# Loading two weight tiles ahead of x, and using both on each block of x: the start of a fused attention layer on one Trainium2 core

## The reference, cut to what matters

```
h = x @ w_in + b_in                      # w_in is 1024 x 5376
q_a, k_a, v_a, gate_a, q_b, k_b, v_b, gate_b, mg_a, mg_b = split(h)
o_a = sliding_window_attention(rope(q_a), rope(k_a), v_a, sinks) * silu(gate_a)
o_b = stick_breaking_attention(q_b, k_b, v_b) * silu(gate_b)
merged = sigmoid(mg_a) * (o_a @ w_up_a) + sigmoid(mg_b) * (o_b @ w_up_b)
out = layer_norm(alpha * x + merged @ w_out)
```

## Time and profile before

| what | value |
|---|---|
| median of 3 timed executions | 861.12 us (857.84 to 861.34) |
| span of the profiled execution | 860.0 us |
| PE busy | 802.8 us, 93% of the span |
| POOL, DVE, ACT busy | 369.3, 465.4, 352.0 us |
| mean granted TensorE clock | 0.982 |
| DMA moved | 51 MB, 59 GB/s over the span |

### The profile page before, as it was taken

The page is one execution under the profiler, slowest core; times in us unless marked ns, Lnnn a source line. Parts: engine busy times, 40 slices in busy tenths (PEclk is TensorE's granted clock), DMA queues, the critical chain, the costliest instruction groups (busy, mean ns, idle before and its releaser), DMA issues.

```text
span 860.0 us, 10173 instructions
## 1 busy us (share of the span) xinstructions
PE 802.8 (93%) x3872; PEld 659.7 (77%) x3872; DVE 465.4 (54%) x620; ACT 352.0 (41%) x644; POOL 369.3 (43%) x321
## 2 busy tenths in 40 slices
PE   8999999999879987998899888999999999999996
PEld 6887877787767776777777666888888888888885
DVE  6377555375886588658865887411202202254453
ACT  7587454543545344534453445312111111144220
POOL 0222111235696669666866687322122222210392
PEclk9999999999999999999999999999999999999999
DMA  9141100013001200120022000111111111124251
GB/s 329 39 123 32 42 27 26 29 48 96 1 25 42 82 1 26 52 71 0 25 59 65 0 26 26 50 50 50 49 50 50 50 49 50 50 72 173 75 204 65
DMA packets 16912, 51.01 MB, mean 59 GB/s; under 512 B 2272, under 2 KB 2272, under 8 KB 16864
## 3 DMA queue, kind: packets, MB, share of 16 engines
q1 hardware_dynamic: 16864, 50.37, 17.7%
HBM read 40.92 MB, written 4.19 MB: 52 GB/s over the span
## 4 chain that ended last, share of the span: by engine, by line
PE 65%; POOL 21%; issue 7%; DVE 4%; ACT 2%; DMA 1%; POOLq 0%; SPq 0%; ACTq 0%; DVEq 0%
PE ps L78 20%; PE ps L80 20%; PE ps L79 20%; POOL keep L313 7%; POOL beta L309 5%; POOL o_t L327 3%; POOL sig_m L322 3%; POOL w_lo L289 2%; PE ps L1139 1%; PE ps L1122 1%; PE ps L1207 1%; PE ps L1150 1%; DVE stick_a L880 1%; ACT w_hi L402 1%; DVE beta L889 1%
## 5 line engine op out<-in xcount | busy, mean ns | idle before, releaser
L289 POOL TENSOR_TENSOR w_lo<-raw,w_hi 128x1024 fp32r<-128x1024 f32 (+1 forms) x53 | 120.2, 2268 | 348.5 <-ACT w_hi L402 347.7
L78 PE MATMUL ps<-x_hi,w_hi 128*128 128x512 f32 x672 | 267.6, 398 | 1.5 <-DVE x_lo L797 1.5
L80 PE MATMUL ps<-x_hi,w_lo 128*128 128x512 f32 x672 | 263.5, 392 | 0.0
L79 PE MATMUL ps<-x_lo,w_hi 128*128 128x512 f32 x672 | 263.3, 392 | 0.0
L78 PEld LDWEIGHTS ps<-x_hi,w_hi 128*128 128x128 f32 x672 | 127.9, 190 | 27.9 <-DVE x_lo L797 2.4
L80 PEld LDWEIGHTS ps<-x_hi,w_lo 128*128 128x128 f32 x672 | 127.0, 189 | 27.6
L79 PEld LDWEIGHTS ps<-x_lo,w_hi 128*128 128x128 f32 x672 | 127.5, 190 | 24.6
L975 DVE TENSOR_TENSOR sig_m<-sig_m,ps 128x512 f32<-128x512 f32 x16 | 10.9, 681 | 168.1 <-PE ps L80 168.1
L402 ACT ACTIVATE w_hi<-raw 128x1024 fp32r<-128x1024 f32 x49 | 51.9, 1060 | 113.3 <-PE ps L80 112.9
L1176 PE MATMUL ps<-ident,beta 128*128 128x128 f32 x288 | 49.9, 291 | 37.8 <-DVE w_t L896 30.1
L567 ACT ACTIVATE w_t<-ps 128x512 fp32r<-128x512 f32 (+1 forms) x96 | 46.6, 490 | 89.5 <-PE ps L1176 89.0
(11 more groups left out here) (112 smaller groups left out, 1183.9 us busy)
## 6 DMA issues: line engine op xcount, KB each, us to landing
raw<-in_w SPq DMA_DIRECT2D x56, 512.0 KB, 3.2
o_t<-in_xt SPq DMA_DIRECT2D x16, 256.0 KB, 5.7
ks<-ks SPq DMA_DIRECT2D x16, 256.0 KB, 4.3
raw<-in_xn SPq DMA_DIRECT2D x8, 512.0 KB, 3.5
out<-o_t SPq DMA_DIRECT2D x16, 256.0 KB, 2.0
raw<-in_w SPq DMA_DIRECT2D x4, 256.0 KB, 5.5
ka<-ka SPq DMA_DIRECT2D x4, 256.0 KB, 4.3
o_t<-in_cos SPq DMA_DIRECT2D x1, 512.0 KB, 5.2
```

The source lines that it names most:

```text
L78: pe.matmul(out, w_hi, x_hi, start=first, stop=False)
L79: pe.matmul(out, w_hi, x_lo, start=False, stop=False)
L80: return pe.matmul(out, w_lo, x_hi, start=False, stop=last)
L289: pool.tensor_tensor(w_lo[:, n % 2, cols], raw[:, n % 2, cols], w_hi[:, n % 2, cols].bitcast(F32), ALU.subtract).then_inc(lo_first if part ...
```

## The change

The first halves of tiles 0 and 1 are now the first two DMAs, ahead of all of x, and their second halves go out together before block 2. ACT and DVE split them in that order. On PE a new function `first_tiles(h)` waits for each block of x and multiplies it with K_A and then with V_A, in two PSUM banks that fill side by side; the order K_A, V_A, K_A, V_A over the halves becomes both on half 0, both on half 1. What follows, and what waits for it, is untouched.

```
-            sp.dma_start(raw[:, 0, 0:HALF], w[0][:, 0:HALF]).then_inc(first_in[0], 16)
+            for n in range(2):
+                sp.dma_start(raw[:, n, 0:HALF], w[n][:, 0:HALF]).then_inc(first_in[n], 16)
             for h in range(2):
                 cols = slice(HALF * h, HALF * (h + 1))
                 for k in range(KT):
                     if h == 0 and k == 2:
-                        sp.dma_start(raw[:, 0, HALF:D], w[0][:, HALF:D]).then_inc(raw_in[0], 16)
+                        for n in range(2):
+                            sp.dma_start(raw[:, n, HALF:D], w[n][:, HALF:D]).then_inc(raw_in[n], 16)
                     sp.dma_start(o_t[:, k, cols], xt[k][:, cols]).then_inc(x_in[KT * h + k], 16)
                 if h == 0:
-                    sp.dma_start(raw[:, 1, 0:HALF], w[1][:, 0:HALF]).then_inc(first_in[1], 16)
-                    sp.dma_start(raw[:, 1, HALF:D], w[1][:, HALF:D]).then_inc(raw_in[1], 16)
...
             first_weights_hi(0, 0)
+            first_weights_hi(1, 0)
             for h in range(2):
                 for k in range(KT):
                     if h == 0 and k == 2:
                         first_weights_hi(0, 1)
+                        first_weights_hi(1, 1)
                     act.wait_ge(x_in[KT * h + k], 16)
...
-                if h == 0:
-                    first_weights_hi(1, 0)
-                    first_weights_hi(1, 1)
...
+            def first_tiles(h):
+
+                xs = slice(HALF * h, HALF * (h + 1))
+                for k in range(KT):
+                    pe.wait_ge(x_lo_done, KT * h + k + 1)
+                    for n in (K_A, V_A):
+                        if h == 0 and k == 0:
+                            pe.wait_ge(first_lo, n + 1)
+                        if h == 0 and k == 4:
+                            pe.wait_ge(lo_done, n + 1)
+                        wk = slice(P * k, P * (k + 1))
+                        last = mma3(pe, ps[:, 2 * n + h, :], w_hi[:, n, wk], w_lo[:, n, wk], x_hi[:, k, xs],
+                                    x_lo[:, k, xs], k == 0, k == KT - 1)
+                        if k == KT - 1:
+                            last.then_inc(half_done, 1)
+
             for h in range(2):
-                for n in (K_A, V_A):
-                    chunk(n, 2 * h)
-                    chunk(n, 2 * h + 1)
+                first_tiles(h)
```

More of the change, by code:

```diff
@@ L791, in _ @@
             first_weights_lo(0, 0)
+            first_weights_lo(1, 0)
             for h in range(2):
@@ L795, in _ @@
                         first_weights_lo(0, 1)
+                        first_weights_lo(1, 1)
                     dve.wait_ge(x_hi_done, KT * h + k + 1)
@@ L798, in _ @@
                                       ALU.subtract).then_inc(x_lo_done, 1)
-                if h == 0:
-                    first_weights_lo(1, 0)
-                    first_weights_lo(1, 1)
             dve.wait_ge(const_in, 32)
```

## The result

| | before | after |
|---|---|---|
| first comparison, median | 859.48 us (4 runs) | 865.62 us (4 runs) |
| ratio | | 1.007, 95% interval 1.0042 to 1.0097 |
| the same kernel again, 5 rounds | 859.8 us | 865.6 us |
| ratio | | 1.0071, interval 1.0055 to 1.0088 |
| span of the profiled execution | 860.0 us | 861.8 us |

The change makes the kernel slower by 0.7%, 6.1 us. 865.0 was forecast, against 861.12 then shown for the kernel before. With more executions of it that one came to 858.2 to 859.8, so the change costs more than the 3.9 to 4.5 us that were forecast. A time and a span are not the same number: in every execution for which both are known the time is 1.7 to 1.8 us above the span (863.51 and 861.8 in the changed kernel's profiled execution). The 860.0 that served as the forecast's lower base was a span and no second estimate of the time.

The account below looks back on a forecast made before the run. PE was taken to bound the kernel, busy for 93% of the span. Start +0.1, wait +3.2 and clock +1.2 made +4.5 us, on 860.0 or 861.12; 865.0 us was forecast, range 863 to 866.5.

Parts of the forecast that it names:

- The wait behind it: Before Q_A (tile 2), PE waits 3.2 us for POOL's w_lo, since tile 0's slot comes free too late.
- What PE waits for elsewhere: PE's waits before the change: 37.6 us in the stick-breaking stage, 1.5 at line 1139, 1.17 and 0.34 for x.
- The covers behind it: After Q_A's start, V_A's eviction and the next tile's weight_hi stay hidden, by 3 us and more.
- The clock after the wait: PE's low clock following the wait before Q_A costs +1.2 us, between bounds of 0 and 1.7.
- Start +0.1: First two tiles: PE starts at 7.9, not 5.64, and ends at 31.4 against 31.32, +0.1 us.
- the gain at the front is nil: First two tiles: time saved by never waiting for x equals what PE's later start costs.
- The landing: First DMAs: block 0 of x, now third transfer, lands at 6.46 us; the other bound was about 4.8.
- The same fall at the same place: First tiles on PE: the clock falls near 9.19 us as before, costing some 1.7 us again.
- Quiet start: First tiles: block 0 lands at 4.8, no clock fall at 9.3; about 863 us; chance 0.13.
- Clock twice: A second low-clock stretch, in the first tiles or after the wait: +1.7 us more, 867; chance 0.12.
- Absorbed: Later waits, at line 1139 and line 1176, absorb Q_A's delay, leaving 1 to 2 us: 862; chance 0.07.
- faster: Stick-breaking stage: low-clock stretches move onto pauses, 1.7 us each; three fewer give -0.6, four 859; chance 0.06.

Follow-up runs that it names:

- both with halves: The changed kernel with tile 2's hi and lo parts made in halves of 512 columns, ratio 1.0039; the same with 36 warm-up transposes, ratio 1.0017.
- the long warm-up: The changed kernel with 36 warm-up transposes in place of 16, ratio 1.0048 to the kernel before.
- half 1 alone: The kernel before, DMA order and half 0 untouched, with K_A and V_A interleaved only on half 1 of x: ratio 1.0067.

## Why the prediction was right, and where it was off

**The wait behind it: right.** 3.2 us were forecast. From the last start of V_A's matmuls, 32.26, and its 0.23 to 35.67 are 3.18; the profile counts 3.02 of it as idle. All six profiles with half 1 interleaved and tile 2 made whole have 3.0, both with halves have 1.5, and of the six others five have none. It hid behind V_A's 5.44 us before, and the change left 0.68 of them.

**What PE waits for elsewhere: read with one gap.** The stick-breaking stage has another 6.6 us of waits, at line 1207 in 13 pieces, beside the 37.6 that the prediction named. It changes no term.

**The covers behind it: right.** `weight_hi(Q_A + 1)` and the eviction of V_A were in time, no further wait appears on line 78, and the delay reaches the keys stage whole (4.48 us there, 4.35 at Q_A).

**The clock after the wait: right in kind, a little over.** I took 1.2 of 0 to 1.7. Of the six profiles with the 3.0 us wait, three show 1.2 GHz within a microsecond of Q_A's start and three, the changed kernel's among them, don't. Q_A's 48 matmuls take 12.6, 12.65 and 13.84 us in the first three and 11.02 in the others, so the low clock costs 1.0 on average. Of the two with 1.5 us of wait none shows it. So the drop is not certain, as one sentence of the prediction had it. A low clock behind the long wait and none behind the short one fits the halves' 2.7 us for 1.5 of wait, but it is argued, not shown: six profiles are few, and the other executions have no timelines.

**The start: mis-sized.** The term "Start +0.1" is the step that failed, and with it "the gain at the front is nil". By the ratios the start costs 2.0 to 2.7 us: the DMA order alone 2.4, half 0 with it 2.7, and the long warm-up takes 2.0 back from the changed kernel. The profiles show three parts, each an average of few executions:

- *The landing.* Block 0, third, was forecast to land at 6.46. In the changed kernel's first profile it landed at 6.66, but in the nine profiles that have it third at 6.66 to 7.78, on average 7.4: +0.9.
- *The clock.* "The same fall at the same place" was forecast, at a cost of 1.7. The low clock is there from the first matmul and lasts for 6 to 12 of them in the six profiles with 16 or 26 warm-ups. K_A and V_A take 1.5 to 2.6 us longer than their 21.8, on average 2.0 (2.6 in the changed kernel): +0.3. The prediction named the hole of 2.2 us in front of them and gave it no weight, since it compared only how much PE worked before the clock fell.
- *The base.* V_A's end at 31.32 was that of a single execution, which had the low clock. With the same DMAs and the same half 0, the profile of half 1 alone has no low clock at the start, and V_A ends at 29.96 there: the average of the two is 0.7 lower.

V_A ends at 32.49 in the changed kernel's first profile, 1.2 later than in the kernel before, and at 32.6 on average over the six profiles. With its three corrections the term is 0.1 + 0.9 + 0.3 + 0.7 = 2.0, an estimate from these few profiles.

**The sum.** 0.1 + 3.2 + 1.2 = 4.5 was forecast. With 2.0 for the start and 1.0 for the clock behind the wait it is 2.0 + 3.2 + 1.0 = 6.2, and 6.1 is measured. That agreement is no proof: the 2.0 is the least of the three values for the start, and half 1 alone came to 5.8 (4.0 to 7.4), where 3.2 + 1.0 makes 4.2. The absolute time, 865.6 against 865.0, is closer than the terms, and that is luck: the base of 861.12 was 1.6 us above the 859.48 of the comparison, and the cost was forecast too low by about as much.

**The chances.** They leaned the other way: 0.55 on a change of less than 0.5% and 0.40 on slower by more. Measured is 0.7%, with an interval from 0.42 to 0.97% in the first comparison and from 0.55 to 0.88% in the second.

**The rivals.** Quiet start: no; block 0 landed at 6.6 to 7.8 in every kernel that has it third, and the clock was low behind it whenever PE had stood still for 2.3 us or more. Clock twice: in part; both places can have the low clock, as the profiles with 26 warm-ups and with block 0 second do. Absorbed and faster: the one profiled pair shows 2.5 us given back in the stick-breaking stage, with four low stretches where the kernel before has six; the medians show nothing of it.

**Open.** Why moving block 0 back to second place helps with half 1 in the old order (1.0003 against 1.0032) and not with both halves interleaved (1.0071 and 1.0071). And what half 1 alone costs beyond the wait and its clock.

## What to carry to other kernels

With two slots, what hides the preparation of the next tile is the work left on the other tile at the moment that the slot comes free. Two tiles that share each block of input come free together, and then nothing hides it: 0.68 us were left of 5.44. So two tiles that are interleaved have to go back to one after the other before the next tile is due. Interleaving where the input is late (half 0) cost nothing that these runs show, but gained nothing either (1.0003 and 0.9999 at best). And a PE that waits for its first input pays twice, once in time and once at 1.2 GHz; dummy transposes up to the first matmul cover the second: 20 more of them took 2.0 us off the changed kernel.

## What the hardware showed that was not expected

- The first transfers of a program don't land evenly. The second was there by 4.1 to 5.5 us in the profiles that have x there, the third in thirteen of fourteen at 6.46 to 8.15 and in one by 6.2, whether it carried x or weights; after that one came each 0.69 us in the kernel before.
- With PE idle for 2.3 to 3.6 us before its first matmul, it started at 1.2 GHz in all six such profiles (0.43 us apart); with transposes until then, or with a hole of up to 1.4 us, it started at 2.4 GHz in seven of eight (0.23 apart). The eighth is the changed kernel with block 0 second, at 1.2 GHz after a hole of 0.80. The Trainium skill (TensorE: Matmul & The Clock Gate, Part 1) has the throttled state as the default, lifted by activity; these runs agree, but don't tell why that one began low.
- The recorded clock can be missing at the start of a profile: 1.00 was shown for stretches where the matmuls were 0.43 us apart.
